# The second half of every expert weight unit is issued by ScalarE instead of SyncE

## What is computed

```python
def _swiglu(h, w_gate, w_up, w_down):
    return (jax.nn.silu(h @ w_gate) * (h @ w_up)) @ w_down

def _moe(h, router_w, router_b, exp_gate, exp_up, exp_down):
    logits = (h @ router_w).astype(jnp.float32) + router_b.astype(jnp.float32)
    top_val, top_idx = lax.top_k(logits, TOP_K)
    wts = jax.nn.softmax(top_val, axis=-1)
    ...
    for e in range(N_EXPERTS):
        y = y + combine[..., e:e + 1] * _swiglu(h, exp_gate[e], exp_up[e], exp_down[e])
```

## Time and profile before

| what | value |
|---|---|
| median of three runs | 1867.89 us (1864.06 to 1867.90) |
| profiled execution | 1866.44 us, of which the span of the profile is 1864.5 us |
| PE / DVE / ACT / POOL busy over the span | 91% / 67% / 53% / 5% |
| DMA | 436.58 MB, mean 234 GB/s |
| stretch from 1200 to 1800 us (experts 1 to 7, one tile each) | PE 98%, DVE 89%, ACT 78% busy, DMA 370 GB/s |

### The profile page before, as it was taken

The page is one execution under the profiler, slowest core; times in us unless marked ns, Lnnn a source line. Parts: engine busy times, 40 slices in busy tenths (PEclk is TensorE's granted clock), DMA queues, the critical chain, the costliest instruction groups (busy, mean ns, idle before and its releaser), DMA issues.

```text
span 1864.5 us, 20706 instructions
## 1 busy us (share of the span) xinstructions
PE 1688.8 (91%) x7867; PEld 1394.9 (75%) x7867; DVE 1250.4 (67%) x1518; ACT 991.6 (53%) x1322; POOL 88.2 (5%) x99
## 2 busy tenths in 40 slices
PE   6889988999989988899799998999999999999890
PEld 4777767778768767898677777888887888888780
DVE  5575446655454356766745455999898989898885
ACT  5762354243323243343434434777777777777770
POOL 0003200110000000000000000000000000000003
PEclk8999989899999998999899999999999999999995
DMA  8553244387444335457235556999999999999993
GB/s 306 192 162 116 67 136 131 102 288 253 138 145 137 111 113 179 141 179 243 98 114 180 181 170 228 374 374 382 374 365 356 365 374 375 373 374 374 351 333 113
DMA packets 205227, 436.58 MB, mean 234 GB/s; under 512 B 13375, under 2 KB 46762, under 8 KB 205098
## 3 DMA queue, kind: packets, MB, share of 16 engines
q1 hardware_dynamic: 195050, 398.20, 61.1%
q0 software_dynamic: 8352, 30.42, 4.8%
q10 hardware_dynamic: 1696, 6.29, 0.8%
HBM read 426.59 MB, written 20.86 MB: 240 GB/s over the span
## 4 chain that ended last, share of the span: by engine, by line
PE 73%; DVE 10%; DMA 7%; ACT 5%; issue 4%; POOL 1%; SPq 0%; DVEq 0%; ACTq 0%; POOLq 0%
PE ps L511 22%; PE ps L513 21%; PE ps L512 21%; DVE w_lo L434 5%; ACT w_hi L428 3%; DMA raw<-in_exp_gate 2%; DMA raw<-in_exp_up 2%; PE ps L1157 1%; PE ps L695 1%; PE ps L696 1%; ACT hf L1418 1%; DMA raw<-in_w_mod 1%; DMA raw<-in_exp_down 1%; PE ps L723 1%; PE ps L924 1%
## 5 line engine op out<-in xcount | busy, mean ns | idle before, releaser
L434 DVE TENSOR_TENSOR w_lo<-raw,w_hi 128x1024 fp32r<-128x1024 f32 (+1 forms) x760 | 894.6, 1217 | 262.6 <-ACT w_hi L428 254.6
L428 ACT CAST w_hi<-raw 128x1024 fp32r<-128x1024 f32 (+1 forms) x760 | 767.5, 1047 | 414.2 <-PE ps L513 275.1
L511 PE MATMUL ps<-w_hi,gT_hi 128*128 128x512 f32 x792 | 316.8, 400 | 19.1 <-issue 8.7
L513 PE MATMUL ps<-w_hi,gT_lo 128*128 128x512 f32 x792 | 311.0, 393 | 0.0
L512 PE MATMUL ps<-w_lo,gT_hi 128*128 128x512 f32 x792 | 310.5, 392 | 0.0
L511 PE MATMUL ps<-w_hi,prodT_hi 128*128 128x512 f32 x528 | 212.9, 403 | 8.8 <-DVE prod_dense L2134 5.2
L513 PE MATMUL ps<-w_hi,prodT_lo 128*128 128x512 f32 x528 | 208.2, 394 | 0.0
L512 PE MATMUL ps<-w_lo,prodT_hi 128*128 128x512 f32 x528 | 208.1, 394 | 0.0
L511 PEld LDWEIGHTS ps<-w_hi,gT_hi 128*128 128x128 f32 x792 | 150.0, 189 | 52.7 <-issue 11.7
L513 PEld LDWEIGHTS ps<-w_hi,gT_lo 128*128 128x128 f32 x792 | 149.8, 189 | 32.3
L512 PEld LDWEIGHTS ps<-w_lo,gT_hi 128*128 128x128 f32 x792 | 150.1, 189 | 29.5
(11 more groups left out here) (356 smaller groups left out, 1861.2 us busy)
## 6 DMA issues: line engine op xcount, KB each, us to landing
raw<-in_exp_gate SPq DMA_DIRECT2D x176, 512.0 KB, 5.7
raw<-in_exp_up SPq DMA_DIRECT2D x176, 512.0 KB, 5.7
raw<-in_exp_down SPq DMA_DIRECT2D x176, 512.0 KB, 5.3
raw<-in_w_mod SPq DMA_DIRECT2D x96, 512.0 KB, 4.6
y_rows<-in_exp_up POOLq DMA_DIRECT2D x8, 1536.0 KB, 27.6
raw<-in_w_in_conv SPq DMA_DIRECT2D x24, 512.0 KB, 6.1
raw<-in_ffn_gate SPq DMA_DIRECT2D x22, 512.0 KB, 5.3
raw<-in_ffn_up SPq DMA_DIRECT2D x22, 512.0 KB, 5.7
```

The source lines that it names most:

```text
L428: nc.scalar.copy(w_hi[:, s, cols], raw[:, n % RAW, cols]).then_inc(sem("w_hi_ready"), 1)
L434: nc.vector.tensor_tensor(w_lo[:, s, cols], raw[:, n % RAW, cols], w_hi[:, s, cols].bitcast(F32), ALU.subtract).then_inc(sem("w_ready"), 1)
L511: nc.tensor.matmul(out, a[0], b[0], start=start, stop=False)
L513: return nc.tensor.matmul(out, a[1], b[0], start=False, stop=stop)
```

## The change

SP keeps part 0 of every expert unit. Part 1 is issued by ACT, in a new function `act_load`, which is called right behind the casts of unit u + 2 and loads part 1 of unit u + 4. It waits for the same semaphore and the same count as SP did: DVE has done with both parts of unit u + 1. The first eight units of the first expert stay with SP whole.

```diff
+LOADED_BY_SP = 8
...
+        def act_load(act, u, e):
+
+            if u >= FFN_UNITS:
+                u, e = u - FFN_UNITS, e + 1
+            if e == N_EXP or (e == 0 and u < LOADED_BY_SP):
+                return
+            n = U_MOE + u
+            nk, src = weight_unit(t, n, e)[1]
+            cols = unit_parts(n)[1]
+            act.wait_ge(sem("w_ready"), val(2 * (n - RAW) + 2, 2 * FFN_UNITS, e))
+            act.dma_start(raw[:, n % RAW, cols].rearrange("p (k n) -> p k n", k=nk), src
+                          ).then_inc(sem(f"raw_landed{n % RAW}_1"), 16)
...
-            def load(n, e=None):
+            def load(n, e=None, which=(0, 1)):
                 for (nk, src), (part, cols) in zip(weight_unit(t, n, e), enumerate(unit_parts(n))):
+                    if part not in which:
+                        continue
...
-                    load(U_MOE + u, e)
+                    load(U_MOE + u, e, (0,) if e or u >= LOADED_BY_SP else (0, 1))
...
                     split_in_loop(act, act_split, u, e)
+                    if u:
+                        act_load(act, u + AHEAD + 2, e)
...
                 split_in_loop(act, act_split, FFN_UNITS, e)
+                act_load(act, FFN_UNITS + AHEAD + 2, e)
```

## The result

| | median | range | runs |
|---|---|---|---|
| before | 1867.89 us | 1864.06 to 1867.90 | 3 |
| changed | 1911.39 us | 1907.07 to 1923.71 | 4 |

The ratio is 1.0252, with a 95% interval of 1.0211 to 1.0293: the change makes the kernel 2.5% slower, 43.5 us, and the time lies above the range of 1859 to 1884 us. A further run of the kernel before, of 1994.77 us, fell into a slower state of the chip and is left out.

What follows compares the result with a forecast made beforehand. PE was taken to bound most of the expert stage, the ring of three slots close behind. All terms were 0 but 2 us for the gather: 1866.4 us became 1868.4, stated as 1869 us, range 1859 to 1884.

Steps and rivals of the forecast that it cites:

- the reserve: Expert-stage loads: 4.0 parts in flight where 1.8 would do, so an issue could be 3.1 us late without harm.
- The wait that ACT gets: ACT's wait for DVE before its issue: no stop, load 0.3 to 0.4 us later, under the reserve; 0 us.
- SP's issues, 0: SP's queue loses 256 issues: worth nothing, since SP was waiting for DVE anyway; 0 us.
- ACT's issues, 0: ACT's queue gains 256 issues, 91 us of it, taken to run under the cast ahead; 0 us.
- ACT held: Rival: each issue holds ACT's queue, 0.46 us per chain pass through a cast, loads later; 1881 or 1869 us; chance 0.09.
- ACT's wait, 0: ACT's wait for DVE's subtraction before issuing part 1: already over when reached, load slightly later without cost; 0 us.
- The gather, +2 us: Gather on POOL's queue beside two load queues, PE waiting at its transposes: between 0 and 4 us, middle taken, 2 us.
- Code, -5 to +5 us: More code on ACT: a stop at a change of expert may go or come, -5 to +5 us, taken as 0.
- The rival of late loads: Rival at the ring of slots: part 1 lands late, 11 us, with the gather's 4 us 1881 us; chance 0.24.
- Its own test: For part 1 loads: late loads decide once median issue to landing plus the delay is over about 6.1 us.
- The simpler sign: Sign that the forecast is wrong: a landing of part 1 over 6.1 us after its issue.
- Better fed: Rival: the second queue fills gaps in the DMA engines, gate and up loads land sooner, 6 us saved, about 1860 us; chance 0.17.

Runs made afterwards that it cites:

- e5: Kernel before, SP issuing all loads, but part 1 waits until part 1 two units earlier landed and that unit's part 0 is cast: 1875.49 us, ratio 1.0053.
- e2: Changed kernel with ACT's issue between the two casts of a unit instead of behind them: 1884.74 us, ratio 1.0107 to the kernel before.
- m1: No computation, only 512 KB loads, on one or two queues with set numbers in flight: 387 GB/s with 4 on one queue, 234 with 2.
- e6: Kernel before, SP issuing all loads, but part 1 waits for the end of the cast of part 1 two units earlier: 1893.22 us, ratio 1.0159.
- e3: Kernel before, SP issuing all loads, plus a 512-byte DMA by ACT in place of each load it issues in the changed kernel: 1863.6 us, ratio 0.9992.
- e7: Kernel before with four slots from the second expert on, one queue, unused three-tile version left out: 1855.01 us, ratio 0.9952.
- m3: Only the ring of loads, casts and subtractions, without TensorE, eight stretches varying queues, unit kinds, other work and slots: 1.33 to 1.50 us a part.
- e8: Changed kernel with four slots from the second expert on, ACT loading one unit further ahead, three-tile version left out: 1851.86 us, ratio 0.9939 to the kernel before.

## Why the prediction was wrong

**The step that failed** is the reserve: "One alone needs 2.6 us, so 1.8 in flight would already keep the engines busy. The difference, 2.2 parts or 3.1 us, is what an issue can be late". The 2.6 us were a lone store; a lone load of the size takes 3.62 us, and 1, 2, 3 and 4 loads in flight bring 144, 234, 313 and 387 GB/s. Between the last two, the 370 GB/s that the kernel used need 3.8 in flight, and it had 3.9 (409 loads of 5.76 us each in the mean, over 600 us). So by these rates the reserve was about 0.1 to 0.2 parts, some 0.2 us by estimate, not 3.1. PE at 98% stood beside a DMA at 370 of 387 GB/s, with three slots between them. The term that rested on it, 0 for a load that goes out late (*The wait that ACT gets*), costs 0.5%, or 10 us, where nothing else is changed (e5).

**The larger part was no term at all.** A second queue of loads I weighed only for the gather; for the loads beside each other I put it at nothing, and no row stood behind that. I had taken over the Trainium skill's sentence ("DMA: Bandwidth & Descriptors", section "Issuing engines are not separate DMA queues") that starting DMAs from several engines saves issue time and nothing else; that ACT's issues are free agrees with it, but it doesn't say that a second queue is free, and the measurement decides. A second queue without lateness costs at most 1.1% (e2, which has ACT's wait for DVE in it), lateness alone 0.5% (e5), and both together 2.5%, more than their sum. What the two do together, the runs show: the loads change from an even row into groups of four that end in close pairs. In the timelines a load into a free slot then stands in ACT's queue behind a cast that waits for a landing; that this is what keeps the groups going is argued from them and from e2, which takes the lateness away and has few pairs, and no run shows it by itself. Only one part of that was in my text: I asked whether ACT would wait for DVE (it hardly does) and took "0.3 to 0.4 us" for the delay from two issues that fell well. The wait that counts is that of the cast ahead.

Fewer loads in flight don't seem to be the main thing. This is an estimate, from the time that each kernel spends at each number in flight (1200 to 1780 us), weighed with m1's rates on one queue: the kernel before comes to 370 GB/s, as measured, and the changed one to 366, where 349 is measured. With m1's 360 for four in flight on two queues, where 8 of 64 landings end a close pair, the changed one comes to 348. The weighing is rough: for e5 it gives 372 where 362 is measured, for e6 345 where it is 355.

Point by point:

- *SP's issues, 0*: right, SP waits 527.8 us.
- *ACT's issues, 0*: right. From 1200 to 1800 us 57% of them begin within 0.1 us of the start of a cast, as at 1547.46 us above, and most others within 0.1 us of DVE's subtraction that they wait for; e3 gives 0.9992. The rival "ACT held" falls with it.
- *ACT's wait, 0*: right as far as DVE goes (3.0 us). Its delay of the load, 0.60 us in the mean, was under-sized (forecast: 0.3 to 0.4 us), and the "0" behind it rested on the reserve.
- *The gather, +2 us*: it lands after 6.5 us in the median, and PE waits 0.3 us once. The term is 0, not 2.
- *Code, -5 to +5 us*: ACT's stop of 6.05 us is gone; no such wait is left in its list of 1200 to 1800 us. Beside 44 us it doesn't show.
- *The rival of late loads* had the place, the ring of slots, and the sign, at 15 us instead of 43.5. Its own test, issue to landing plus the delay over about 6.1 us in the median, just came true: for part 1 it is 6.14 us, before 5.84. The simpler sign, a landing of part 1 over 6.1 us, did not: the landings are 5.5 to 6.0 us. A median hides groups of four; one load in ten of part 1 now takes over 7.4 us to land, before 6.6.
- *Better fed* is what four slots bring, not two queues: in e7, on one queue, the casts' waits for loads fall from 55 to 4 us. How much of its 0.5% is that and how much the missing stop is open.

Left open: what tips the ring. In m3 it went over with the other work alone (stretch 3) and with other units alone (1), and with both it came back soon (6). One queue lands every load after the one issued before it; with two, 6 of 371 change places, and 36 end within 0.5 us of another, always one of each queue. Why two loads of different queues end together was not tested. The Trainium skill, "DMA: Bandwidth & Descriptors", section "Queues, rings and completion order", has each DMA engine take packets in turn from the queues that have work; by that rule the heads of two queues would share the engines and could end close to each other. The traces agree in part: m1 has 8 close pairs at 2 + 2 in flight, but 1 at 3 + 3 and none at 1 + 1.

## What to carry to other kernels

Before a load is moved to another engine's queue, look at what stands ahead of it there: a load into a free slot should not wait behind an instruction that itself waits for a load. Take the reserve of a load stream from rates at a known number in flight, not from the latency of one transfer, and look at the spread of the landings, not their median. Where the DMA engines and the engine that they feed are both nearly full, as here (370 of 387 GB/s, PE 98%), try a further slot before a further queue: here it made the choice of queue harmless (e7, e8).

## What was not expected of the hardware

- One queue of 512 KB loads: 144, 234, 313, 387 GB/s with 1, 2, 3, 4 in flight, and 387 with 5 and 6. Two queues with 1 each: 234, with 2 each some 360, with 3 each 389.
- Two queues of loads through three slots had two states at one and the same code (m3): 387 to 394 GB/s in an even row, 314 to 350 in groups, for 90 us and more at a time.
- A DMA issue behind a cast on ACT's queue whose own wait is over goes out when the cast begins, not when it ends (0.01 us after, at 1541.11 us), and 256 of them cost the kernel nothing that can be measured (e3, 0.9992).
